# Two blocks on one NeuronCore: retention's values, gate and output in other PSUM banks, the last head's attention ahead of its gate, and a norm's steps spread singly

## What is computed

```python
# first block, layer 0: retention, 4 heads, dk 256, dv 512
h = rms_norm(x) * (1 + sc1) + sh1
q, k, v, g = split(h @ ret_w_in)                  # q and k turned by rotary(pos)
o = causal, decayed (q k^T) v                     # per head, with gamma_h ** (n - m)
x = x + g1 * (normed(o) * silu(g)) @ ret_w_out    # o centred and normed per head and token
# second block, layer 0: an "even" mixer, once for x, once for ctx (256 tokens)
p = modulate(ctx) @ even_w_in                     # Fourier part | gelu(u, v)
ctx = ctx + cg1 * concat(fourier, u * sgu(v)) @ even_w_out
x = x + g2 * conv_ffn(modulate(x))                # its norm is the "second norm", f2
```

## Time and profile before

| what | value |
|---|---|
| median of 3 runs | 3098.82 us (3096.73 to 3102.41) |
| the profiled execution: its own time, its span | 3094.08 us, 3092.3 us |
| granted TensorE clock, mean | 0.971 of full |
| busy: TensorE, VectorE, ScalarE, POOL | 96%, 58%, 36%, 13% |
| mean of one: split low (VectorE), split high (ScalarE) | 1.30 us, 1.05 us |
| one norm operation of 128x512: VectorE, ScalarE's high part | 0.75 us, 0.72 us |
| ScalarE's eviction of 128x256 and of 128x512 (vv, O) | 0.38 us, 0.60 us |
| a fp32 product of 512 columns (two records on TensorE) | 0.86 us |
| attend: the products of one O bank | 2.16 us |

### The profile page before, as it was taken

How to read it: one execution, slowest core, us unless ns; L and a number is a source line. 1 busy time by engine, 2 the same in 40 slices (tenths; PEclk the granted TensorE clock), 3 DMA queues, 4 the chain that set the end, 5 groups by cost and what they waited for, 6 DMA issues and landing times. The chain is left out here.

```text
span 3092.3 us, 37685 instructions
## 1 busy us (share of the span) xinstructions
PE 2954.3 (96%) x15108; PEld 2457.2 (79%) x15108; DVE 1803.3 (58%) x2518; ACT 1100.4 (36%) x1569; POOL 399.9 (13%) x384
## 2 busy tenths in 40 slices
PE   5999998999999999999999999999999999999999
PEld 4777776788888878888768787888998887778887
DVE  7355445866556566766545488664774436554443
ACT  3222234323333333323423332334553436542322
POOL 0000001376671100000001000000000102100000
PEclk9999998999999999999989899999999999999999
DMA  6443322355557555554324356553563431123332
GB/s 263 130 143 109 102 96 83 118 173 178 170 184 244 185 165 157 156 151 141 118 62 122 110 174 190 187 184 111 162 186 108 141 97 57 31 85 101 96 96 82
DMA packets 123312, 421.01 MB, mean 136 GB/s; under 512 B 21521, under 2 KB 21521, under 8 KB 122369
## 3 DMA queue, kind: packets, MB, share of 16 engines
q1 hardware_dynamic: 102096, 369.67, 38.7%
q0 software_dynamic: 11056, 41.95, 4.1%
q10 hardware_dynamic: 9984, 6.97, 0.7%
HBM read 401.31 MB, written 19.86 MB: 136 GB/s over the span
## 5 line engine op out<-in xcount | busy, mean ns | idle before, releaser
L121 DVE TENSOR_TENSOR wl<-raw,wh 128x1024 fp32r<-128x1024 f32 x506 | 658.2, 1301 | 582.3 <-ACT wh L118 560.8
L112 PE MATMUL bk<-HH,wh 128*128 128x512 f32 x2176 | 862.4, 396 | 23.0 <-DVE HL L133 13.4
L112 PE MATMUL bk<-HL,wh 128*128 128x512 f32 x2176 | 855.6, 393 | 0.0
L112 PE MATMUL bk<-HH,wl 128*128 128x512 f32 x2176 | 854.8, 393 | 0.0
L118 ACT ACTIVATE wh<-raw 128x1024 fp32r<-128x1024 f32 x506 | 531.0, 1050 | 436.3 <-PE bk L112 429.1
L112 PEld LDWEIGHTS bk<-HH,wh 128*128 128x128 f32 x2176 | 414.2, 190 | 116.7 <-DVE HL L133 15.5
L112 PEld LDWEIGHTS bk<-HH,wl 128*128 128x128 f32 x2176 | 413.8, 190 | 87.8
L112 PEld LDWEIGHTS bk<-HL,wh 128*128 128x128 f32 x2176 | 414.4, 190 | 85.7 <-issue 0.7
L124 DVE CUSTOM_DVE_ANT_0 ttr<-ar,cB 128x1024 f32<-128x1024 f32 x240 | 309.1, 1288 | 2.2
L112 PE MATMUL bk<-gh,wh 128*128 128x512 f32 x704 | 275.3, 391 | 6.1 <-DVE glE L121 5.5
L112 PE MATMUL bk<-gh,wl 128*128 128x512 f32 x704 | 274.6, 390 | 0.0
(11 more groups left out here) (303 smaller groups left out, 3896.3 us busy)
## 6 DMA issues: line engine op xcount, KB each, us to landing
raw<-in_wts_dram SPq DMA_DIRECT2D x506, 512.0 KB, 3.6
ar<-in_ada_dram SPq DMA_DIRECT2D x176, 512.0 KB, 4.3
first<-in_ada_dram SPq DMA_DIRECT2D x16, 512.0 KB, 15.3
F_d<-CA POOLq DMA_DIRECT2D x8, 512.0 KB, 5.2
E_d<-stg POOLq DMA_DIRECT2D x16, 256.0 KB, 5.1
M_d<-K_d POOLq DMA_DIRECT2D x8, 512.0 KB, 10.4
EB<-E_d POOLq DMA_DIRECT2D x8, 512.0 KB, 6.0
EB<-M_d POOLq DMA_DIRECT2D x8, 512.0 KB, 7.4
```

What stands on the lines that cost most here:

```text
L112: return Nothing() if self.e is None else self.e.matmul(*a, **k)
L121: return Nothing() if self.e is None else self.e.tensor_tensor(*a, **k)
```

## The change

Retention's values go to banks 6, 7, 0, 1 and its gate, attention products and output to 2, 3, 0, 1. The last head has its attention right behind its values; mean and variance then come as in the other heads, the mean inside the gate, the variance and the transposes inside head 2's output. f2's steps: one per output in the last four of the input stage, and five in the output stage of the context half.

```diff
@@ -630,6 +630,8 @@
+        VB, GB = [6, 7, 0, 1], [2, 3, 0, 1]
...
@@ ret_pe, qkv
-                                  lambda k, tt: HL[:, k, tt * 128:tt * 128 + 128], xw, [0, 1, 2, 3], lambda tt: (act, ("vv", h, tt))):
+                                  lambda k, tt: HL[:, k, tt * 128:tt * 128 + 128], xw, VB, lambda tt: (act, ("vv", h, tt))):
...
             def gate(h):
-                run(gemm(e, ("g", h), w_ret(h) + 8, 4, 8, hh, hl, xw, L, [0, 1, 2, 3], lambda m: (act, ("sg", h, m))))
+                return gemm(e, ("g", h), w_ret(h) + 8, 4, 8, hh, hl, xw, L, GB, lambda m: (act, ("sg", h, m)))
...
             def mean(h):
                 claim(e, 4)
-                if h < 3:
-                    e.wait_ge(*pool.of(("osum", h, 3)))
-                    e.matmul(BK[4][:, :], con("one512"), ssq[:, :], start=True, stop=True).then_inc(*pe.up(("mean", h)))
-                else:
-                    for j in range(4):
-                        e.wait_ge(*act.of(("O", h, j)))
-                        mm = e.matmul(BK[4][:, :], con("one512"), r.O[:, j, :], start=(j == 0), stop=(j == 3))
-                    mm.then_inc(*pe.up(("mean", h)))
+                e.wait_ge(*pool.of(("osum", h, 3)))
+                e.matmul(BK[4][:, :], con("one512"), ssq[:, :], start=True, stop=True).then_inc(*pe.up(("mean", h)))
...
@@ ret_pe, the order
             qkv(3, lambda: mean(2), lambda: var(2), lambda: turned(2))
-            gate(3)
             attend(3)
-            for m in out(2):
+            for m in gate(3):
                 if m == 1:
                     mean(3)
-                if m == 5:
+            for m in out(2):
+                if m == 0:
                     var(3)
-            turned(3)
+                if m == 3:
+                    turned(3)
             run(out(3))
...
@@ ret_act, the order
                 vv(h + 1)
                 if h < 2:
                     out(h)
-                gate(h + 1)
+                    gate(h + 1)
                 attend(h + 1)
-            hi(e, last_unit(("out", 2), 1, 4) + 2)
-            squares(3)
-            hi(e, last_unit(("out", 2), 5, 4) + 2)
+            gate(3, lambda m: squares(3) if m == 2 else None)
+            hi(e, last_unit(("out", 2), 0, 4) + 2)
             root(3)
             out(2)
             high(3, base[("out", 3)])
...
@@ ret_vec, the order
                 project(h)
                 if h < 3:
                     out(h - 1)
-                gate(h)
+                    gate(h)
                 decayed(h)
-            for m in range(2):
+            for m in range(4):
+                lo(e, last_unit(("g", 3), m, 8) + 2)
+                if m == 2:
+                    centred(3)
+            for m in range(8):
                 lo(e, last_unit(("out", 2), m, 4) + 2)
-                add_to(e, ("out", 2), m, m % 4, X, L, 0, 2)
-            centred(3)
...
+                add_to(e, ("out", 2), m, GB[m % 4], X, L, 0, 2)
+                if m == 1:
                     inverse(3)
             gated(3, base[("out", 3)])
...
@@ ret_pool
-            for h in range(3):
+            for h in range(4):
...
@@ -2176,6 +2162,8 @@
         EARLY = {0: (0,), 3: (1,), 4: (2, 3), 5: (4, 5), 6: (6, 7), 7: (8, 9)}
+        SPREAD_IN = {0: (0,), 4: (1,), 5: (2,), 6: (3,), 7: (4,)}
+        SPREAD_OUT = {1: (5,), 2: (6,), 3: (7,), 4: (8,), 5: (9,)}
...
-            even_act(e, v_c, "e", lambda e, m: [norm_step_act(e, n_f2, 6, i) for i in EARLY.get(m, ())])
+            even_act(e, v_c, "e", lambda e, m: [norm_step_act(e, n_f2, 6, i) for i in SPREAD_IN.get(m, ())],
+                     lambda e, m: [norm_step_act(e, n_f2, 6, i) for i in SPREAD_OUT.get(m, ())])
...
-            even_vec(e, v_c, lambda e, m: [norm_step_vec(e, n_f2, i) for i in EARLY.get(m, ())])
+            even_vec(e, v_c, lambda e, m: [norm_step_vec(e, n_f2, i) for i in SPREAD_IN.get(m, ())],
+                     lambda e, m: [norm_step_vec(e, n_f2, i) for i in SPREAD_OUT.get(m, ())])
```

More of the change, by code:

```diff
@@ L669, in attend @@
                 for j in range(4):
-                    claim(e, j)
+                    claim(e, GB[j])
                     e.wait_ge(*act.of(("vv", h, 3)))
@@ L673, in attend @@
                         e.wait_ge(*vec.of(("st", h, mt)))
-                        mm = e.matmul(BK[j][:, mt * 128:L], r.vv[:, mt, j * 128:j * 128 + 128], r.St[:, mt, :L - 128 * mt],
+                        mm = e.matmul(BK[GB[j]][:, mt * 128:L], r.vv[:, mt, j * 128:j * 128 + 128], r.St[:, mt, :L - 128 * mt],
                                       start=(mt == 0), stop=(mt == 3))
                     mm.then_inc(*pe.up(("o", h, j)))
-                    bank[j] = (act, ("O", h, j))
+                    bank[GB[j]] = (act, ("O", h, j))
             def mean(h):
                 claim(e, 4)
-                if h < 3:
-                    e.wait_ge(*pool.of(("osum", h, 3)))
-                    e.matmul(BK[4][:, :], con("one512"), ssq[:, :], start=True, stop=True).then_inc(*pe.up(("mean", h)))
-                else:
-                    for j in range(4):
-                        e.wait_ge(*act.of(("O", h, j)))
-                        mm = e.matmul(BK[4][:, :], con("one512"), r.O[:, j, :], start=(j == 0), stop=(j == 3))
-                    mm.then_inc(*pe.up(("mean", h)))
+                e.wait_ge(*pool.of(("osum", h, 3)))
+                e.matmul(BK[4][:, :], con("one512"), ssq[:, :], start=True, stop=True).then_inc(*pe.up(("mean", h)))
                 bank[4] = (vec, ("oc", h, 3))
@@ L692, in var @@
                 claim(e, 5)
[L693 to L700, removed]
+                e.wait_ge(*pool.of(("vsum", h, 3)))
+                token_sums(e, 5, ssq, con("one512")[:, 0:1], True, True).then_inc(*pe.up(("var", h)))
                 bank[5] = (act, ("oroot", h))
@@ L709, in out @@
                 return gemm(e, ("out", h), w_ret_out(h), 8, 4, lambda k: r.oh[:, k, :], lambda k: r.ol[:, k, :],
-                            lambda e, k: e.wait_ge(*vec.of(("ol", h, k))), L, [0, 1, 2, 3], lambda m: (vec, ("x", ("out", h), m)))
+                            lambda e, k: e.wait_ge(*vec.of(("ol", h, k))), L, GB, lambda m: (vec, ("x", ("out", h), m)))
             qkv(0)
-            gate(0)
+            run(gate(0))
             attend(0)
@@ L716, in ret_pe @@
             run(out(0))
-            gate(1)
+            run(gate(1))
             attend(1)
@@ L720, in ret_pe @@
             run(out(1))
-            gate(2)
+            run(gate(2))
             attend(2)
             qkv(3, lambda: mean(2), lambda: var(2), lambda: turned(2))
-            gate(3)
             attend(3)
-            for m in out(2):
+            for m in gate(3):
                 if m == 1:
                     mean(3)
-                if m == 5:
+            for m in out(2):
+                if m == 0:
                     var(3)
-            turned(3)
+                if m == 3:
+                    turned(3)
             run(out(3))
@@ L755, in vv, with gate @@
                         e.wait_ge(*pe.of(("o", h - 1, 3)))
-                    e.activation(r.vv[:, tt, :], BK[tt][:, :], ACT.Copy).then_inc(*act.up(("vv", h, tt)))
-            def gate(h):
+                    e.activation(r.vv[:, tt, :], BK[VB[tt]][:, :], ACT.Copy).then_inc(*act.up(("vv", h, tt)))
+            def gate(h, beside=lambda m: None):
                 if h == 1:
@@ L764, in gate @@
                     hi(e, last_unit(("g", h), m, 8) + 2)
+                    beside(m)
                     e.wait_ge(*pe.of((("g", h), m)))
@@ L767, in gate @@
                         e.wait_ge(*vec.of(("ol", h - 1, m)))
-                    e.activation(r.sg[:, m, :], BK[m][:, :], ACT.Silu).then_inc(*act.up(("sg", h, m)))
+                    e.activation(r.sg[:, m, :], BK[GB[m]][:, :], ACT.Silu).then_inc(*act.up(("sg", h, m)))
             def attend(h):
@@ L776, in attend @@
                         e.wait_ge(*act.of(("cos", "rope")))
-                    e.activation(r.O[:, j, :], BK[j][:, :], ACT.Copy).then_inc(*act.up(("O", h, j)))
+                    e.activation(r.O[:, j, :], BK[GB[j]][:, :], ACT.Copy).then_inc(*act.up(("O", h, j)))
             def squares(h):
@@ L781, in squares @@
                     e.wait_ge(*vec.of(("oc", h, j)))
-                    if h < 3 and j == 0:
+                    if j == 0:
                         e.wait_ge(*pe.of(("mean", h)))
@@ L785, in squares @@
                         continue
-                    if h < 3 and j == 3:
+                    if j == 3:
                         e.wait_ge(*pool.of(("vsum", h, 1)))
-                    if h == 3 and j >= 2:
-                        e.wait_ge(*pe.of(("var3", j - 2)))
                     e.activation(pr[j % 2][:, :], r.O[:, j, :], ACT.Square).then_inc(*act.up(("osq", h, j)))
@@ L905, in out @@
                     lo(e, last_unit(("out", h), m, 4) + 2)
-                    add_to(e, ("out", h), m, m % 4, X, L, 0, 2)
+                    add_to(e, ("out", h), m, GB[m % 4], X, L, 0, 2)
```

(11 more changed lines are left out.)

## The result

| | median of the runs | ratio to before, 95% interval | profiled execution: time, span, clock |
|---|---|---|---|
| before, run beside it | 3097.78 us (3096.01 to 3102.41) | | 3094.08, 3092.3, 0.971 |
| changed | 3055.26 us (3048.48 to 3059.96) | 0.9859 (0.9836 to 0.9882) | 3053.06, 3051.2, 0.976 |

The kernel is 42.5 us faster by the medians, 41.1 by the spans. The forecast was 41.7 less, and 3057 us.

What follows compares the result with a forecast made beforehand. TensorE, with work in 96% of the span, bounds the kernel; its idle time and lower clock can be won. -20.4 - 8.0 - 8.7 + 1.0 - 7.4 + 1.8 = -41.7 us, giving 3057 us; 8 in 10 range 3047 to 3067.

Steps and rivals of the forecast that it cites:

- part 1: Retention's values in banks 6, 7, 0, 1: four waits on `tm` and slow clock behind them go, -20.4 us.
- part 2: Gate and output in banks 2, 3, 0, 1: three waits on `vv` and one slow clock window go, -8.0 us.
- late next: Behind the first values unit, transposes need VectorE's reciprocal: 0.2 us of margin, no wait, but the next limit.
- The other margin: Head 1's output needs VectorE's last `ol` only in its fourth k step, 9 matmuls on: margin 0.3 us.
- Rival A: Retention's margins of 0.2 and 0.3 us fail; waits return on the reciprocal or `ol`: 8 us, 3065, chance 15%.
- The last head, 3: Start of head 2's output to start of head 3's falls from 36.9 to 28.2 us: -8.7, against +1.0 for `St`.
- what would show it: Signs in the later profile: `tm`, `vv`, `Acce` waits gone, small `St` wait, head 3's four `ol` waits unchanged in size.
- The context half, 4: Norm steps spread over input and output stages: `Acce` wait and slow clock go, -7.4 us, against +1.8 in the output stage.
- the price of POOL's hold: Context half's output stage: POOL's adds hold VectorE's differences, split low 0.45 us later in four periods, +1.8 us (0 to 3.5).
- B: Only half of part 4: each of five output-stage periods grows fully, 7.5 us instead of 1.8; 3063, chance 6%.
- C: Slower: weight splits become retention's limit over 68 units, sign turning from 0.62 us per unit; 3111 at 0.8, chance 2%.
- D: Values still wait since bank 0 is claimed too; parts 1 and 2 are lost, result 3085, chance 2%.

Runs made afterwards that it cites:

- e2_all_banks: The kernel before with values in banks 6, 7, 0, 1 and gate, attention products and output in 2, 3, 0, 1, nothing else changed: 3067.95 us, ratio 0.9910.
- e3: The kernel before with only the last head's new order, banks 0 to 3 everywhere: 3086.96 us, ratio 0.9969.
- e5_low_first: The changed kernel with VectorE's difference ahead of its scaling in the context half's output stage: 3054.17 us, ratio 0.9855 against the kernel before.
- e1: The kernel before with only the values moved to banks 6, 7, 0, 1: 3079.83 us, ratio 0.9952.

## Why the prediction was right, point by point

**The banks, 1 and 2.** -28.4 was forecast, -29.3 measured. The 20.9 us of idle time in it, waits and overlaps, are gone as counted. The clock gave a little more than the 7.5 us forecast: the stage of e2_all_banks is 29.3 us shorter, its recorded waits and their overlaps 20.7, and the 8.6 that remain are matmuls that run faster (clock 0.99 over the stage, 0.97 before). Parts 1 and 2 are not independent, which the forecast did not say: 2.9 us of part 1 appear only with part 2. What was "late next" was seen rightly: behind head 3's first values unit VectorE's reciprocal and TensorE's transposes stand at

```profile
358.77 0.17 DVE L142 RECIPROCAL nst<-nst 128x4 f32<-128x4 f32 x1
```

```profile
359.14 0.60 PE L115 MATMUL bk<-cst,nst 128*128 128x128 f32 x4
```

so the margin is 359.14 - 358.94 = 0.2 us, as worked out, and no wait arose. The other margin held as well: head 1's output starts at 273.53, its tenth matmul comes 9 x 0.227 us later, at 275.57, and the last `ol` ends at 275.25, 0.3 us ahead. Rival A, which had 15%, falls with them: no wait on a reciprocal, and none on `ol` in the outputs of heads 0 to 2.

**The last head, 3.** From the start of head 2's output to head 3's it takes 439.58 - 412.60 = 27.0 us, and the mean, about 0.9, now lies in the gate; the forecast had 28.2 with the mean in it. The last 3.8 of it were taken right: a wait of 3.64 and an overlap of 0.16. Before it was 3.20, with the transposes in its shadow. The wait on `St` is 0.76, forecast 1.0. With the banks turned already the order takes 403.53 - 396.04 = 7.5 us off the stage up to head 3's output, forecast 7.7. With the old banks (e3) it is 8.4, but that includes the wait on `vv` that the forecast counts in part 2.

One point that "what would show it" named here failed, with no price. The four `ol` waits were to keep their size and are 3.64, 1.70, 1.06 and 2.61 instead of 3.20, 1.00, 1.06 and 2.61. The second is longer because TensorE comes earlier: both before and after, the second step begins 2.6 us behind the first, for VectorE's chain sets it. From the first of these waits to the fourth it takes 9.58 us before and 9.59 after. A wait of this kind grows as the waiting engine gets quicker, and its size says nothing of a loss. The 0.7 us by which head 3's output is longer lie behind the fourth wait, in 116 matmuls that take 30.85 us instead of 30.15, at a clock of 0.83 instead of 0.84.

**The context half, 4.** -5.6 was forecast ("shorter by 5 to 6"), -7.6 measured, and this is the part that is furthest off. The wait on `Acce` and its clock went as forecast. The term that was mis-sized is the price of POOL's hold, +1.8 us, "some 0.45 us later, four periods". A difference is held 0.50 us, but in e5_low_first, without the hold, VectorE still waits for the split's high part: 0.18 us recorded, and 0.09 more, by which its records overlap where it waits for nothing. So 0.27 us of the hold fell into idle time, and the period grew by 0.23, not 0.45. The wait at the end grew by 0.6 us (2.51 against 1.93) where 3 to 4 us were said. The e5 run puts the term at 1.0 us, within the 0 to 3.5 that the text gave. The other 1.2 us can't be told from what varies in this stage: with the old order it took 90.5 to 93.8 us in four kernels, in single executions, so the gain of 7.6 is itself uncertain by that much.

**Rivals.** B wanted periods longer by 1.5 us; they are longer by 0.23. C falls with the weight splits: TensorE's waits on them are 11.6 us after 11.0, and 396 us of retention run with two waits below 1 us. C's count of 68 units is wrong: the kernel has 16 per head, 64 in all, so its bound is 41.7 / 64 = 0.65 us per unit, which changes neither its mechanism nor its chance. D falls with e1 and e2.

**The total.** Forecast -41.7 in the profiled execution, measured -41.1 (spans). This closeness is partly luck: the touched stages gave 2.6 us more than forecast, and the others gave 3.0 back.

## What to carry to other kernels

Look at which PSUM bank a stage writes first, and who reads that bank at that moment: reordering two lists of banks took 29 us off here, half again as much as the 19.7 us of waits that it removed, since behind four of the seven waits a stretch ran partly at 1.2 GHz. When one list is turned, turn the lists behind it as well, or the wait moves on. Then look for what stands in a chain only by the order of the program: two products per tile that needed no buffer gave 11 us more in their stage.

## What the runs showed of the hardware

- **A stage of unchanged work has two lengths.** In ten profiled executions the state-space mixer takes 195.2 to 196.3 us in five and 200.8 to 204.1 in the other five, with the same matmuls. Windows on TensorE over that stage of e3_last_head and of e5_low_first:

```profile
920.18:1116.34 196.16, 185.04 (x1245) 0.93 0.62 204
```

```profile
893.67:1097.78 204.11, 191.44 (x1244) 0.89 0.60 194
```

  The lengths differ by 8.0 us. The clock is 0.89 where it was 0.93, and TensorE's busy time is 6.4 us longer; the other 1.5 are idle time. What decides between the two was not tried. The difference is as large as the smaller effects studied here, and may be why medians of four runs did not resolve 3 us.
- **The length of a wait alone does not tell the clock behind it.** In the changed kernel the waits of 0.82 and 0.76 us lie in a stage whose granted clock is 1.00. In e2_all_banks a wait of 0.62 us has half clock behind it. There the clock fell before the wait, while TensorE did the variance's 32 products of one column each (windows on TensorE, the first two inside those products, the third behind the wait):

```profile
430.48:432.50 2.02, 2.02 (x20) 1.00 0.00 0
432.50:434.00 1.50, 1.50 (x9) 0.54 0.00 0
436.04:439.50 3.46, 3.46 (x8) 0.51 0.78 173
```

  The kernel before has the same at this place: 1.00 in the first 1.87 us of those products, and 0.50 over 3.41 us behind the wait of 1.55. In e1_values_banks, on the other hand, waits of 3.30 us kept 1.00. And the same wait does not always cost the same: the third of the values' waits, 2.99 us at 272.27, had 1.00 behind it, and in e3_last_head the same wait, 2.98 us at 270.43, had 0.63 over 4.57 us. The forecast's price of the clock, a sum over seven waits, came out near the measured one; the price of a single wait can't be taken from one execution.
- **The hold costs less than the overlap.** The difference started 0.05 us behind an add of 0.74 us, so they overlap by 0.69; it took 0.50 us longer than alone, and the add kept its 0.74 us.
